# First loads, first hidden tiles and last post norms of a transformer backbone layer, put in another order

## The reference

```python
x = x + sincos_2d(rows, GRID_W, d)
m = (silu(c) @ w_ada + b_ada).reshape(bsz, 9, d)        # latent modulation
mc = (silu(c_ctx) @ w_ada + b_ada).reshape(1, 9, d)     # context modulation
x  = post_norm(x,  swiglu(modulate(x, m, 0),  ffn1_w_in, ffn1_w_out), m[:, 2],  0.5, ln_gain[0], ln_bias[0])
xc = post_norm(xc, swiglu(modulate(xc, mc, 0), ffn1_w_in, ffn1_w_out), mc[:, 2], 0.5, ln_gain[0], ln_bias[0])
y, _ = token_mixer(modulate(x, m, 1), modulate(xc, mc, 1), ...)   # GLA and HGRN2 scans, both directions
x = post_norm(x, y, m[:, 5], 1.0, ln_gain[1], ln_bias[1])
x = post_norm(x, swiglu(modulate(x, m, 2), ffn2_w_in, ffn2_w_out), m[:, 8], 0.5, ln_gain[2], ln_bias[2])

def modulate(x, m, i): return layer_norm(x) * (1 + m[:, 3*i]) + m[:, 3*i+1]
def post_norm(x, y, gate, weight, gain, bias): return layer_norm(ALPHA * x + weight * gate * y, gain, bias)
```

## Time and profile before

| | us |
|---|---|
| median of 3 runs | 1563.05 (1562.62 to 1564.52) |
| the profiled execution's own time | 1560.92 |
| its span, first to last instruction | 1559.1 |
| TensorE busy | 1438.5 (92%) |
| VectorE busy | 711.1 (46%) |
| ScalarE busy | 511.7 (33%) |
| GpSimd busy | 81.7 (5%) |
| mean granted TensorE clock | 0.962 |

### The profile page before, as it was taken

One profiled execution on the slowest core, in us unless ns is written; L12 is line 12 of the kernel. 1 busy time (PEld: TensorE's weight loads), 2 busy tenths in 40 slices (PEclk: granted clock), 3 DMA queues, 4 the chain that ended last, 5 costly groups with the idle time before them and its releaser, 6 DMA issues.

```text
span 1559.1 us, 18192 instructions
## 1 busy us (share of the span) xinstructions
PE 1438.5 (92%) x7613; PEld 1164.3 (75%) x7613; DVE 711.1 (46%) x894; ACT 511.7 (33%) x697; POOL 81.7 (5%) x86
## 2 busy tenths in 40 slices
PE   5899999999999998999999999997748999999994
PEld 2677777777789998787777778886647887888783
DVE  4344323433336765453155456676663233332335
ACT  3234211222213555424253354553323222122220
POOL 3000000000000000000011011110000000000000
PEclk9899999999999999999999999998978999999997
DMA  9555456555435664450121112213322322433221
GB/s 290 185 154 157 144 180 188 164 162 155 156 108 136 172 180 122 152 186 17 42 67 41 27 28 55 55 55 135 108 54 79 111 90 86 109 82 107 75 74 54
DMA packets 201313, 177.06 MB, mean 114 GB/s; under 512 B 6522, under 2 KB 166792, under 8 KB 201232
## 3 DMA queue, kind: packets, MB, share of 16 engines
q1 hardware_dynamic: 191056, 137.97, 30.3%
q0 software_dynamic: 9856, 37.78, 7.2%
q10 hardware_dynamic: 320, 0.14, 0.0%
HBM read 173.78 MB, written 2.10 MB: 113 GB/s over the span
## 4 chain that ended last, share of the span: by engine, by line
PE 82%; DVE 7%; ACT 5%; issue 4%; DMA 1%; ACTq 0%; POOL 0%; DVEq 0%; POOLq 0%
PE ps L1563 25%; PE ps L1564 23%; PE ps L1565 23%; ACT w_hi L652 2%; PE ps L1587 2%; DVE w_lo L1044 1%; PE ps L1940 1%; PE ps L1938 1%; DVE stats L1059 1%; ACT hfull L671 1%; DVE xl L1096 1%; PE ps L1603 1%; PE ps L1923 1%; DVE xl L1089 1%; PE ps L1887 1%
## 5 line engine op out<-in xcount | busy, mean ns | idle before, releaser
L1044 DVE TENSOR_TENSOR w_lo<-w_raw,w_hi 128x2048 fp32r<-128x2048 f32 (+3 forms) x113 | 250.6, 2219 | 375.1 <-ACT w_hi L652 374.8
L1563 PE MATMUL ps<-h_hi,w_lo 128*128 128x512 f32 (+1 forms) x1104 | 397.9, 360 | 16.5 <-DVE h_lo L1082 10.8
L1564 PE MATMUL ps<-h_lo,w_hi 128*128 128x512 f32 (+1 forms) x1104 | 392.6, 356 | 0.0
L1565 PE MATMUL ps<-h_hi,w_hi 128*128 128x512 f32 (+1 forms) x1104 | 392.4, 355 | 0.0
L652 ACT ACTIVATE w_hi<-w_raw 128x2048 fp32r<-128x2048 f32 (+3 forms) x113 | 209.5, 1855 | 543.1 <-PE ps L1565 541.8
L1563 PEld LDWEIGHTS ps<-h_hi,w_lo 128*128 128x128 f32 x1104 | 210.4, 191 | 57.9 <-DVE h_lo L1082 11.6
L1565 PEld LDWEIGHTS ps<-h_hi,w_hi 128*128 128x128 f32 x1104 | 210.0, 190 | 32.3
L1564 PEld LDWEIGHTS ps<-h_lo,w_hi 128*128 128x128 f32 x1104 | 210.3, 190 | 30.3
L1563 PE MATMUL ps<-h_hi,half_lo 128*128 128x512 f32 (+1 forms) x272 | 103.8, 382 | 3.6 <-DVE gate L1407 3.3
L1564 PE MATMUL ps<-h_lo,half_hi 128*128 128x512 f32 (+1 forms) x272 | 99.8, 367 | 0.0
L1565 PE MATMUL ps<-h_hi,half_hi 128*128 128x512 f32 (+1 forms) x272 | 99.6, 366 | 0.0
(11 more groups left out here) (212 smaller groups left out, 1868.7 us busy)
## 6 DMA issues: line engine op xcount, KB each, us to landing
w_raw<-ffn_w_in SPq DMA_DIRECT2D x132, 512.0 KB, 5.2
ada_block<-w_ada POOLq DMA_DIRECT2D x36, 1024.0 KB, 5.9
w_raw<-ffn_w_out SPq DMA_DIRECT2D x60, 512.0 KB, 4.1
half_raw<-w_mix_in SPq DMA_DIRECT2D x48, 256.0 KB, 3.2
w_raw<-w_mix_out SPq DMA_DIRECT2D x12, 512.0 KB, 4.7
w_raw<-w_mix_in SPq DMA_DIRECT2D x8, 512.0 KB, 4.4
w_raw<-ffn_w_out SPq DMA_DIRECT2D x12, 256.0 KB, 3.8
xl<-x SPq DMA_DIRECT2D x4, 512.0 KB, 7.3
```

The lines of the kernel that those rows point to most:

```text
L1044: nc.vector.tensor_tensor(lo, raw, hi.bitcast(F32), ALU.subtract).then_inc(s_lo[s], 1)
L1563: nc.tensor.matmul(dst, s_low, m_high, start=start, stop=False)
L1564: nc.tensor.matmul(dst, s_high, m_low, start=False, stop=False)
L1565: return nc.tensor.matmul(dst, s_high, m_high, start=False, stop=stop)
```

## The change

Six edits, all at the two ends of the program.

1. The small rows. Position rows and identity become the first two transfers of ScalarE's queue, with a semaphore of their own; `c`, `c_ctx` and the two GLA biases follow. `b_ada`, the HGRN logits and the two gains move to SP's queue, between token tiles 1 and 2. On TensorE the position products come before the transpose of the rows, and the first two turns before the first block's products.
2. The slots. `xc` and the gain and bias rows (now one tile) serve as slots 4 and 5, so blocks 4 and 5 are issued after the positions of tile 1, and blocks 6 and 7 wait for the products of blocks 0 and 1. The context load waits for six block products.
3. The splits. ScalarE makes the high part of weight 0 before pair 0's modulation and that of weight 1 before pair 1's. VectorE makes each low part before the pair's `first_low`.
4. The last two pairs. TensorE makes pair 3's modulation first and then multiplies job 0 by pairs 2 and 3, and after it job 1 by pairs 2 and 3.
5. The HGRN constants (logit differences, exponential) move behind the last pair, and two activation table loads are written out.
6. The tail. `last_half` takes the last half-output in the order of `LAST_ORDER` (step, tile), and VectorE does each tile's post norm right after its add; the statistics of the first 512 columns are taken after the half before.

The diff, cut to its core:

```diff
+LAST_ORDER = [(0, 0), (0, 1), (0, 2), (0, 3), (1, 0), (1, 1), (2, 0), (2, 1), (1, 2), (2, 2), (1, 3), (2, 3)]
...
+        for block in (xc, gain_bias_b):
+            ada_slots.append(block[:, :, :].rearrange("p a (b c) -> p (a b) c", c=256))
...
@@ SP
             sp.dma_start(pcol[:, :], t["k_pcol"]).then_inc(s_pcol, 16)
-            for i in range(1, TL):
+            tokens(1)
+            for row, n, name in ((R_BADA, 72, "b_ada"), (R_LB, 16, "hgrn_lb_logits"), (R_GAIN, 1, "gla_norm_gain"),
+                                 (R_GAIN + 1, 1, "hgrn_norm_gain")):
+                sp.dma_start(rows[row:row + n, :], t[name]).then_inc(s_const, 16)
+            for i in range(2, TL):
                 tokens(i)
             load(0)
             load(1)
...
                 if i == 3:
+                    sp.wait_ge(s_fada, ADA_SLOTS)
@@ GpSimd
-                elif m >= 4:
-                    pool.wait_ge(s_fada, m - 3 if m < ADA_FIRST else ADA_FIRST)
+                elif m >= ADA_SLOTS:
+                    pool.wait_ge(s_fada, m + 1 - ADA_SLOTS if m < ADA_FIRST else ADA_FIRST)
@@ ScalarE
-            act.wait_ge(s_lbd, 1)
-            nc.scalar.activation(small[:, 16:32], small[:, 16:32], ACT.Exp).then_inc(s_lbe, 1)
-            act.wait_ge(s_zero, 8)
+            nc.scalar.preload_act_table_set("sqrt_and_others")
+            act.wait_ge(s_zero, 1)
...
             take_turned(TL - 1)
+            split_hi(0)
             act.wait_ge(s_xnT, TL)
             for pair in range(4):
...
-                if pair < 2:
-                    split_hi(pair)
+                if pair == 0:
+                    split_hi(1)
+            act.wait_ge(s_lbd, 1)
+            nc.scalar.activation(small[:, 16:32], small[:, 16:32], ACT.Exp).then_inc(s_lbe, 1)
+            act.wait_ge(s_zero, 8)
@@ VectorE
+            def half_statistics(i, h):
+
+                dve.wait_ge(s_yev, Y["L2", 1, h, i] + 1)
+                ins = nc.vector.bn_stats(last_stats[:, i, 6 * h:6 * h + 6], xl[:, i, h * W:(h + 1) * W])
+                if h:
+                    link(ins)
+                    nc.vector.bn_aggr(mv[:, i, :], last_stats[:, i, :]).then_inc(s_stat, 1)
+                    dve.wait_ge(s_stat, STAT["post", "lat", 2, i] + 1)
...
                                     add_output((tag, part, half, tile), gate)
+                                    if (tag, part, half) == ("L2", 1, 0):
+                                        half_statistics(tile, 0)
+                                    if (tag, part, half) == ("L2", 1, 1):
+                                        half_statistics(tile, 1)
+                                        post_center("lat", 2, tile)
+                                        post_scale("lat", 2, tile)
...
                 first_modulation(pair)
+                if pair < 2:
+                    split_lo(pair)
                 first_low(2 * pair)
                 first_low(2 * pair + 1)
-                if pair < 2:
-                    split_lo(pair)
@@ TensorE
+            def last_half():
...
+                for s, tile in LAST_ORDER:
+                    i = JOB["L2", "out", part, half, s]
...
+                    ready(i)
...
+                    for k in range(kk):
+                        ins = product(ps[:, y_bank(("L2", part, half, tile)), :], hid_hi[:, k0 + k, c],
+                                      hid_lo[:, k0 + k, c], hi[:, k, :], lo[:, k, :], k0 + k == 0, k0 + k == tiles - 1)
+                    if s == len(OUT_STEPS[tiles]) - 1 and tile < TL - 1:
+                        ins.then_inc(s_y, 1)
+                    elif tile == TL - 1:
+                        ins.then_inc(s_done[i % 2], 1)
...
             first_pair_turn(0)
-            for pair in range(1, 4):
+            for pair in range(1, 3):
                 first_ada(2 * pair)
                 first_ada(2 * pair + 1)
                 first_pair_turn(pair)
-                first_products(pair - 1)
-            first_products(3)
+                for j in range(2):
+                    first_products(j, pair - 1)
+            first_ada(6)
+            first_ada(7)
+            first_pair_turn(3)
+            for j in range(2):
+                for pair in (2, 3):
+                    first_products(j, pair)
```

More of the change, by code:

```diff
@@ L358, in build @@
         s_done = [sem(f"slot{s}_products_done") for s in range(2)]
-        s_ada_first = [sem(f"ada_slot{i}_loaded") for i in range(4)]
+        s_ada_first = [sem(f"ada_slot{i}_loaded") for i in range(ADA_SLOTS)]
         s_ada_loaded = sem("ada_loaded")
@@ L526, in _ @@
             sp.dma_start(ones[:, :], t["k_ones"]).then_inc(s_ones, 16)
-            for m in range(4):
-                sp.wait_ge(s_ada_first[m], 32)
+            for m in range(ADA_SLOTS):
+                sp.wait_ge(s_ada_first[m], 32 if m + ADA_SLOTS < ADA_FIRST else 16)
             for i in range(2, len(JOBS)):
@@ L578, in _ @@
                 nc.gpsimd.memset(a2[d][:, :], 0.0).then_inc(s_a2z, 1)
-            for i in range(TL):
-                positions(i)
-            for m in range(4, ADA_FIRST):
+            for m in range(ADA_SLOTS, ADA_FIRST):
                 ada(m)
@@ L1550, in _ @@
             ffn("L2", ("lat", 2))
[L1551 to L1556, removed]
         @block.tensor
@@ L1684, in out_half @@
                 return b
+            def last_half():
+                part, half = 1, 1
+                tiles = FFN_PARTS["L2"][part]
+                base = HID["L2", part, 0]
+                hid_hi, hid_lo = hid_last
+                pe.wait_ge(s_hid, base + tiles)
+                for s, tile in LAST_ORDER:
+                    i = JOB["L2", "out", part, half, s]
+                    k0, kk = out_k("L2", part, s)
+                    hi, lo = (x.rearrange("p (k c) -> p k c", c=W) for x in weights(i)[1:])
+                    ready(i)
+                    if s == 0:
+                        pe.wait_ge(s_yev, Y["L2", part, 1, 0] - (3 if tile == 3 else 4))
+                    c = slice(tile * P, (tile + 1) * P)
+                    for k in range(kk):
[5 more added lines that the diff above has]
+                        ins.then_inc(s_done[i % 2], 1)
             def ffn(tag):
@@ L1695, in ffn @@
                     for half in range(2):
-                        b = out_half(tag, part, half, b)
+                        if (tag, part, half) == ("L2", 1, 1):
+                            last_half()
+                        else:
+                            b = out_half(tag, part, half, b)
             def between(tag, b):
@@ L1744, in first_turn, with first_products @@
                 ins.then_inc(s_fturned, 1)
[L1746 to L1750, removed]
-                    for u in range(2):
[L1752 to L1758, removed]
+            def first_products(j, pair):
+                i = JOB["L1", "in", 0, j]
+                ready(i)
+                for k in (2 * pair, 2 * pair + 1):
+                    pe.wait_ge(s_hk, k + 1)
+                    for u in range(2):
+                        ins = project(i, 256, u * P, P, [(2 * j + u, 0, SEQ, 0)], k, k + 1)
+                if pair == 3:
+                    ins.then_inc(s_done[i % 2], 1)
+            pe.wait_ge(s_prow, 32)
             pe.wait_ge(s_spread, 1)
@@ L1761, in _ @@
                 nc.tensor.matmul(ps[:, i, :], spread[:, i * P:(i + 1) * P], prow[:, :], start=True, stop=True).then_inc(s_posps, 1)
+            pe.wait_ge(s_const, 16 * 8)
+            nc.tensor.transpose(cols_ps, rows[0:N_ROWS, :], ident[0:N_ROWS, 0:N_ROWS]).then_inc(s_cols_ps, 1)
+            first_turn(0)
+            first_turn(1)
             pe.wait_ge(s_silu_c, 1)
+            first_ada(0)
+            first_turn(2)
+            first_ada(1)
+            first_turn(3)
             pe.wait_ge(s_quad, 1)
[L1764 to L1767, removed]
             first_pair_turn(0)
-            for pair in range(1, 4):
+            for pair in range(1, 3):
                 first_ada(2 * pair)
```

58 lines of the change are left out of this document (32 added, 26 removed).

## The result

The change takes 1541.8 us (median of 4 runs, 1540.2 to 1543.1) against 1562.8 before in the same comparison: ratio 0.9864, 95% interval 0.9847 to 0.9881, or 21 us less. The forecast was 1546.2. The profiled execution took 1541.49 us (span 1539.7), 19.4 less than the one before (1560.92), where the sum had 16.8.

What follows compares the result with a forecast made beforehand. TensorE, busy 92% of the span, bounds the middle; VectorE alone the tail. Terms -11.8, -1.6 and -3.4 sum to -16.8: 1560.92 profiled becomes 1544.1, and the median, 2.1 above, 1546.2 us; range 1538 to 1552.

Steps and rivals of the forecast that it cites:

- The tail: Last half-output: VectorE's post norms follow each tile without running dry, ending at 1544.2 instead of 1556.07; -11.8 us.
- Six slots: Start, DMA queues: four more blocks follow directly and hold the weights back; weight 0 lands at 37.8 instead of 25.8.
- the 24 that went with that rate: Start: at 436 GB/s transfers finish some 7 us earlier, near 30.4, for a whole gain of about 24 us; chance 0.02.
- From there to job 1: Start, from weight 0's landing: job 1 follows job 0 without a gap, ending at 53.8 instead of 55.43; -1.6 us.
- The first rival: Start: the weights aren't held back, weight 0 lands before 28.3, and the total is 1537 us; chance 0.22.
- Weight splits between the pairs: Start, ScalarE: splitting ahead of each pair's modulation makes it stand still until the weight lands; no separate size.
- Small rows first: Start: tile 1 begins 3.7 us earlier, last turned tile taken at 28.3 instead of 32.0; counted at nothing.
- Pairs 2 and 3: Start, before job 2: TensorE's idle 2.34 us and the lower clock after it go; -3.4 us.
- both signs: Start, job 2: near 78.4 with no idle time ahead, and 1.5 us more from first products at full clock.
- Slower: Start: weight 0 lands after 57.7, so the change loses over 3.1 us; chance 0.02.
- the middle: Between start and tail: the matmuls' own time, left alone by the change, so gains at either end pass through whole.

Runs made afterwards that it cites:

- The tail alone: The kernel before with only the new order of the last half-output and post norms tile by tile: 1549.6 us, ratio 0.9920.
- eight-slot kernel: The changed kernel with eight modulation slots instead of six, two more in the context columns of h: 1545.0 us, ratio 0.9896.
- rows late: The changed kernel with small rows loaded in the old order on ScalarE's queue, position rows last, TensorE's new order kept: 1542.5 us, ratio 0.9881.
- old pairs: The changed kernel with pairs 2 and 3 multiplied in the order of the kernel before: 1547.1 us, ratio 0.9904.
- start alone: The changed kernel with the old last half-output and old loop of post norms: 1554.8 us, ratio 0.9949.
- the wait alone: The changed kernel with four slots, and blocks 4 to 7 held until weight 1 has landed: 1542.0 us, ratio 0.9866.
- the version with order and wait: The changed kernel with four slots, start work reordered on TensorE, ScalarE and VectorE, and blocks 4 to 7 waiting for weight 1: 1536.4 us, ratio 0.9840.
- the order alone: The changed kernel with four slots and start work reordered on TensorE, ScalarE and VectorE, blocks 4 to 7 not waiting for weight 1: 1538.7 us, ratio 0.9849.

## Why the prediction was right, and where it missed

**The tail** (-11.8, measured -11.6). Every step held: tiles 5.26 us apart (5.2), VectorE ready with the third weight at 1511.76, ahead of tile 0's last matmuls, the early half statistics hidden. The tail alone gave 12.5 by the ratio, whose interval (9.5 to 15.3 us) takes this in.

**Six slots** foretold that the weights would be held back at 0.040 MB/us, with weight 0 at 37.8 and weight 1 at 41.4. The rate was exact, the dates 32.8 and 42.4. What failed is the line that blocks 6 and 7 are issued "at about 24 and 26", so that four more blocks "follow directly". They wait for block products 0 and 1, which stand behind turns on TensorE and came late. Besides, the forecast counted nothing between a block's issue and its first packets; for block 6 it was some 4.7 us by estimate (27.6 to about 32.3, as 7 software packets moved from 30 to 32). In the gap weight 0 got through; then the blocks came, and weight 1 was late instead. In the eight-slot kernel, where nothing waits, weight 0 landed at 38.0. The Trainium skill ("DMA: Bandwidth & Descriptors", section "Queues, rings and completion order") has each DMA engine take turns between the queues it has work for, a packet at a time. The trace agrees: 605 packets to 599, and 351 to 353. The flat rate of the section "Anatomy of one DMA" on that page of the Trainium skill (bytes over 436 GB/s) was not borne out here either: 1.35 + 0.18 MB in 4.5 us is 340 GB/s. The gain of 21 us lies nearer to the 24 that went with that rate than to the forecast's 16.8, but for another reason, the gap between the blocks.

**From there to job 1** is the term of the sum that was mis-sized: -1.6 in the forecast, -5.8 measured (55.43 to 49.67), outside its bound of -4. First products came at 40.7 and not 45.8, 5.1 of it from weight 0; weight 1 gave back 0.9 as idle time before job 1; and the clock rose near 45 us, at the end of job 0's first pair rather than at job 1. The first rival was thus half true: the blocks do hold the weights, but not without a gap.

**Weight splits between the pairs** were priced only inside that term. Undoing them alone costs 5.8 us: in the change job 1 waits 0.86 us for its low part and not 3.00, and keeps the clock.

**Small rows first** was to bring the last take to 28.3. It came at 32.08, no earlier than before. The profile shows five reasons. The identity landed at 6.05 (5.4 taken). VectorE's copy of it took 1.47 us and the first `xn` 2.01, where the same instructions take 0.42 and 0.81 otherwise. The columns came at 15.24 instead of 13.6. Two block products still ran between the turns. And the second and third turn took 1.94 and 1.55 us, against 1.10 and 1.06 before. VectorE's lines, and the GpSimd operations beside them:

```profile
6.05 1.47 DVE L1223 COPY gate_b<-ident 8x512 f32<-8x512 f32 x1 [6.05 <-DMA ident<-k_ident]
...
15.24 0.27 DVE L1267 COPY cols<-ps 128x110 f32<-128x110 f32 x1 [2.58 <-PE ps L1812]
...
17.91 2.01 DVE L1237 TENSOR_SCALAR xn<-xl,mv,rstd 128x1024 f32<-128x1024 f32 x1
```

```profile
5.99 1.25 POOL L576 TENSOR_TENSOR xl<-xl,pcol 128x512 f32<-128x512 f32 x1 [0.93 <-DMA pcol<-k_pcol]
...
17.37 1.26 POOL L576 TENSOR_TENSOR xl<-xl,pcol 128x512 f32<-128x512 f32 x1 [1.52 <-DMA xl<-x]
```

The forecast counted this term at nothing because weight 0 was to be later. With the weight at 32.8 the two chains are 0.7 us apart, and the term does count: rows late costs 2.5.

**Pairs 2 and 3** (-3.4) was right in size and cause: from the block product behind job 1's first pair to the mark it is 33.8 us before and 30.2 after. With the old pairs 3.5 us came back, and both signs with it, the idle time and the lower clock after it.

**Slower** had 0.02 and was never near: it needed weight 0 at 57.7. By the profiles the sum was 2.6 us too careful: 4.3 at the start, less 0.2 in the tail and 1.5 in the middle, which run the other way. That the total came within 4.4 us owes something to luck: weight 0's date was 5.0 us off, weight 1's 1.0 the other way, and the middle's loss, which the forecast had at nothing, covered a third of what the start had gained over it.

## What to carry to other kernels

A transfer that is started early takes its share of the DMA engines from whatever is needed first: count packets of both queues, and date each issue by the instruction that releases it, not by the place in the program, and its first packets later still. Where a split or a norm can be made before other work that its reader doesn't wait for, try that before another buffer: here the order of two splits gave 5.8 us and two more slots took 3.4. Undo each part of a bundle once: here one part, the six slots, was worth more taken out than left in.

## What the runs showed of the hardware

- **The granted clock in the mixer differs between executions**, with the same work, by more than several parts of this change are worth. Read from 1020 to 1070 us behind the mark, so that the same stretch of work is compared, it is 0.73 in the three kernels with the longest middles (1432.4 start alone, 1433.0 the wait alone, 1433.5 old pairs), 0.80 in those with 1429.4 to 1430.3, and 0.81 or 0.82 in those with 1427.3 to 1428.1. It isn't the kernel: of the four executions of old pairs, two had a mean granted clock of 0.968 and took 1544.6 and 1545.6 us, the others 0.963 and 0.964 and took 1549.2 and 1548.7. A mark near the edit keeps this out, a median of four does not.
- **An early clock can be worth as much as an early transfer**: 3.2 of the 3.9 us between the version with order and wait and that with the order alone are work at 0.50 of the clock in the one and at 1.00 in the other.
- **Two VectorE instructions took longer beside a GpSimd operation on tensors, others did not.** The copy of the identity (1.47 us) ends 0.28 us after the GpSimd operation that it overlaps. The first `xn` (2.01 us) overlaps one for 0.72 us and ends 1.29 us after it. With the rows late no GpSimd operation on `xl` runs beside these two, and they take 0.41 and 0.81. The addition of the position rows at 15.43 took 0.68 us beside one, no more than elsewhere, and the column copy at 15.24 took 0.27, as before. The Trainium skill ("SBUF — State Buffer", section "Who interferes with whom") says that in some modes the two share a port pair, and one waits until the other's instruction is over. The copy agrees with it; `xn` agrees only in part, as it lost 1.20 us to an overlap of 0.72.
